# A bias table stored during the first norm and loaded in mid-FFN, and one table padded to 128 bytes

## The reference

```
h = x + 1/2 * SwiGLU_1(RMSNorm(x))            # hidden width 2816
u = RMSNorm(h); one projection of u gives queries, latents, indexer, pool input, 3 gates
h = h + W_out( sum_i sigmoid(gate_i) * (branch_i @ W_branch_i) )
h = h + 1/2 * SwiGLU_2(RMSNorm(h))
```

```python
n = jnp.maximum(dist, 0)                      # below 16: the bucket is the distance
large = 16 + (log(n / 16) / log(128 / 16) * 16).astype(int32)   # at most 31
```

## Time and profile before

| | |
|---|---|
| median of 3 runs | 2397.23 us |
| the profiled execution, its span | 2396.16 us, 2394.3 us |
| mean granted TensorE clock | 0.989 |
| PE busy | 2312.5 us (97%) |
| weight loads (beside PE) | 1846.1 us (77%) |
| DVE, ACT, POOL busy | 52%, 23%, 58% |
| DMA | 208.74 MB, 87 GB/s over the span |

### The profile page before, as it was taken

How to read it: one execution, slowest core, us unless ns; L and a number is a source line. 1 busy time by engine, 2 the same in 40 slices (tenths; PEclk the granted TensorE clock), 3 DMA queues, 4 the chain that set the end, 5 groups by cost and what they waited for, 6 DMA issues and landing times.

```text
span 2394.3 us, 31804 instructions
## 1 busy us (share of the span) xinstructions
PE 2312.5 (97%) x10328; PEld 1846.1 (77%) x10328; DVE 1249.8 (52%) x1756; ACT 560.3 (23%) x1038; POOL 1389.6 (58%) x868
## 2 busy tenths in 40 slices
PE   3999999999999999999999999999999999999997
PEld 2788888777877788888778888877777778888875
DVE  2453355478865755225454524636787566440453
ACT  1211112243455221001121101214334532110111
POOL 2566666634434666666666666664344366666663
PEclk8999999999999999999999999999999999999998
DMA  5233223311121322232232332232121122223222
GB/s 136 90 116 95 97 87 98 101 58 66 58 67 49 112 91 89 88 104 85 81 107 96 110 103 91 80 110 80 54 64 61 53 97 89 97 79 105 96 76 73
DMA packets 66482, 208.74 MB, mean 87 GB/s; under 512 B 7352, under 2 KB 9560, under 8 KB 66136
## 3 DMA queue, kind: packets, MB, share of 16 engines
q1 hardware_dynamic: 63600, 202.84, 25.7%
q10 hardware_dynamic: 2792, 4.72, 0.9%
HBM read 203.86 MB, written 3.67 MB: 87 GB/s over the span
## 4 chain that ended last, share of the span: by engine, by line
PE 89%; DVE 7%; DMA 2%; issue 1%; ACT 1%; DVEq 0%; ACTq 0%
PE bank L517 27%; PE bank L519 27%; PE bank L518 27%; DMA bias_rows<-q 1%; PE obank L737 1%; PE sbank L689 1%; PE tbank L710 1%; DVE u1L L1429 1%; DVE picks L1229 1%; DVE picks L1252 1%; DVE tb L1443 1%; PE sbank L684 1%; PE obank L724 1%; DVE top L1227 1%; PE sbank L671 1%
## 5 line engine op out<-in xcount | busy, mean ns | idle before, releaser
L468 POOL TENSOR_SCALAR wH<-raw 128x1024 fp32r<-128x1024 f32 (+3 forms) x432 | 438.2, 1014 | 944.6 <-PE bank L519 926.8
L471 POOL TENSOR_TENSOR wL<-raw,wH 128x1024 fp32r<-128x1024 f32 (+3 forms) x432 | 951.5, 2202 | 36.0
L517 PE MATMUL bank<-u0H,wH 128*128 128x512 f32 x1408 | 563.3, 400 | 6.9 <-POOL wL L471 4.1
L518 PE MATMUL bank<-u0H,wL 128*128 128x512 f32 x1408 | 559.7, 398 | 0.0
L519 PE MATMUL bank<-u0L,wH 128*128 128x512 f32 x1408 | 559.7, 397 | 0.0
L517 PEld LDWEIGHTS bank<-u0H,wH 128*128 128x128 f32 x1408 | 266.1, 189 | 76.5 <-issue 8.5
L518 PEld LDWEIGHTS bank<-u0H,wL 128*128 128x128 f32 x1408 | 266.4, 189 | 65.3 <-issue 1.2
L519 PEld LDWEIGHTS bank<-u0L,wH 128*128 128x128 f32 x1408 | 266.2, 189 | 65.0
L517 PE MATMUL bank<-u1H,wH 128*128 128x512 f32 x704 | 295.7, 420 | 7.5 <-DVE u1L L1429 3.1
L517 PE MATMUL bank<-hidH,wH 128*128 128x512 f32 x704 | 279.6, 397 | 0.7 <-DVE hidL L1132 0.7
L518 PE MATMUL bank<-hidH,wL 128*128 128x512 f32 x704 | 279.1, 396 | 0.0
(11 more groups left out here) (175 smaller groups left out, 2411.0 us busy)
## 6 DMA issues: line engine op xcount, KB each, us to landing
raw<-in_wA SPq DMA_DIRECT2D x176, 512.0 KB, 3.3
raw<-in_wM SPq DMA_DIRECT2D x96, 512.0 KB, 3.3
raw<-in_wB SPq DMA_DIRECT2D x64, 384.0 KB, 3.0
raw<-in_wB SPq DMA_DIRECT2D x64, 320.0 KB, 2.9
raw<-in_wR SPq DMA_DIRECT2D x32, 256.0 KB, 2.6
h<-in_xT ACTq DMA_DIRECT2D x4, 512.0 KB, 6.8
mem<-in_memT SPq DMA_DIRECT2D x2, 1024.0 KB, 6.8
outT<-gate_a SPq DMA_DIRECT2D x4, 512.0 KB, 2.7
```

The lines of the kernel that those rows point to most:

```text
L468: pool.tensor_scalar(wH[:, w, 0:cols], raw[:, slot, 0:cols], 1.0, 0.0, ALU.mult, ALU.add).then_inc(rounded, 1)
L471: pool.tensor_tensor(wL[:, w, 0:cols], raw[:, slot, 0:cols], wH[:, w, 0:cols].bitcast(F32), ALU.subtract).then_inc(split_done, 1)
L517: pe.matmul(dst, a, hi[:, k, :], start=first and i == 0, stop=False)
L518: pe.matmul(dst, b, hi[:, k, :], start=False, stop=False)
```

## The change

Two things are done. The table's way to DRAM and back is cut up: `hot`, `rel` and the table now lie in the memory of `near_bias`; ACT copies the table after the third tile of the first norm and issues the store after the fourth; the issue of `far_bias` stays after the eighth; the wait for the store and the load of `near_bias` move into the first FFN's code, behind the loop over its first 12 hidden tiles, and so run in both layers (DVE's wait counts accordingly). And `far_bias` is declared 32 words wide instead of 8, so that what is declared after it lies 96 bytes further: `cst` at a multiple of 128 bytes, `pr` 32 past one, `rms` to `sg` 64 past one, `u0H` and all that lay 32 past one at a multiple of 128.

```diff
--- before.py
+++ after.py
@@ -73,6 +73,8 @@
 N_SCORES = 3 * IH
 NBIAS = 384
 
+LINE = 128
+
 
 def attention_steps():
 
@@ -207,7 +209,7 @@
         wH = sb("wH", [P, SPLIT_SLOTS, 8 * P], F32R)
         wL = sb("wL", [P, SPLIT_SLOTS, 8 * P], F32R)
         near_bias = sb("near_bias", [P, H, 2 * P])
-        far_bias = sb("far_bias", [P, H])
+        far_bias = sb("far_bias", [P, LINE // 4])
         cst = sb("cst", [P, N_CONST])
         pr = sb("pr", [P, N_PAR])
         rms = sb("rms", [P, T])
@@ -275,8 +277,10 @@
         ones = cst[:, K_ONE:K_ONE + P]
         causal = cst[:, K_CAUSAL:K_CAUSAL + P]
 
-        rel_sb = q[0:BUCKETS, 1, 0:H]
-        bias_table = q[0:H, 2, 0:NBIAS]
+        bias_scratch = near_bias[:, :, :].rearrange("p a t -> p (a t)")
+        hot_sb = bias_scratch[0:BUCKETS, 0:NBIAS]
+        rel_sb = bias_scratch[0:BUCKETS, NBIAS:NBIAS + H]
+        bias_table = bias_scratch[0:H, 4 * P:4 * P + NBIAS]
 
         def masks(qb):
             return causal if qb == 0 else picks[qb][:, :]
@@ -406,8 +410,8 @@
         def _(sp):
             sp.dma_start(cst[:, :], const).then_inc(const_loaded, 16)
 
-            sp.dma_start(q[0:BUCKETS, 0, 0:NBIAS], hot).then_inc(rel_loaded, 16)
-            sp.dma_start(q[0:BUCKETS, 1, 0:H], rel).then_inc(rel_loaded, 16)
+            sp.dma_start(hot_sb, hot).then_inc(rel_loaded, 16)
+            sp.dma_start(rel_sb, rel).then_inc(rel_loaded, 16)
 
             with sp.Fori(0, L) as l:
                 def units(src, per_layer, first, count, cols, unit):
@@ -537,7 +541,7 @@
 
             pe.wait_ge(const_loaded, 16)
             pe.wait_ge(rel_loaded, 32)
-            pe.matmul(sbank[0][0:H, 0:NBIAS], rel_sb, q[0:BUCKETS, 0, 0:NBIAS], start=True, stop=True
+            pe.matmul(sbank[0][0:H, 0:NBIAS], rel_sb, hot_sb, start=True, stop=True
                       ).then_inc(bias_full, 1)
 
             with pe.Fori(0, L) as l:
@@ -845,19 +849,16 @@
                 if k:
                     act.wait_ge(ssq_added, k)
                 act.activation(sq[:, :], h[:, k, :], ACT.Square).then_inc(squared, 1)
-            act.dma_start(far_bias[:, :], bass.AP(tensor=rel.tensor, offset=(BUCKETS - 1) * H,
-                                                  ap=[[0, P], [1, H]])).then_inc(far_loaded, 16)
-            act.wait_ge(bias_full, 1)
-            act.activation(bias_table, sbank[0][0:H, 0:NBIAS], ACT.Copy).then_inc(bias_copied, 1)
-            act.wait_ge(bias_copied, 1)
-
-            act.dma_start(bias_rows, bass.AP(tensor=bias_table.tensor, offset=bias_table.offset,
-                                             ap=[bias_table.ap[0], [0, P], [1, NBIAS]])).then_inc(bias_stored, 16)
-            act.wait_ge(bias_stored, 16)
-
-            act.dma_start(near_bias[:, :, :], bass.AP(tensor=bias_rows.tensor, offset=P - 1,
-                                                      ap=[[NBIAS - 1, P], [P * NBIAS, H], [1, 2 * P]])
-                          ).then_inc(bias_loaded, 16)
+                if k == 2:
+                    act.wait_ge(bias_full, 1)
+                    act.activation(bias_table, sbank[0][0:H, 0:NBIAS], ACT.Copy).then_inc(bias_copied, 1)
+                if k == 3:
+                    act.wait_ge(bias_copied, 1)
+                    act.dma_start(bias_rows, bass.AP(tensor=bias_table.tensor, offset=bias_table.offset,
+                                                     ap=[bias_table.ap[0], [0, P], [1, NBIAS]])
+                                  ).then_inc(bias_stored, 16)
+            act.dma_start(far_bias[:, 0:H], bass.AP(tensor=rel.tensor, offset=(BUCKETS - 1) * H,
+                                                    ap=[[0, P], [1, H]])).then_inc(far_loaded, 16)
 
             with act.Fori(0, L) as l:
                 def ffn(chunk, hid_from, root_n, hi, g, n_from):
@@ -873,6 +874,10 @@
                     with act.Fori(0, HALF[0] // 2) as j:
                         hidden(j, chunk, hid_from)
                     if chunk == 0:
+                        act.wait_ge(bias_stored, 16)
+                        act.dma_start(near_bias[:, :, :], bass.AP(tensor=bias_rows.tensor, offset=P - 1,
+                                                                  ap=[[NBIAS - 1, P], [P * NBIAS, H], [1, 2 * P]])
+                                      ).then_inc(bias_loaded, 16)
 
                         act.wait_ge(mem_loaded, l * 16 + 16)
                         for k in range(KD):
@@ -1209,7 +1214,7 @@
                     dst = kc[:, i, :] if i < 2 else vc[:, i - 2, :]
                     dve.tensor_copy(dst, bank[i][:, 0:M]).then_inc(evacuated, 1)
 
-                dve.wait_ge(bias_loaded, 16)
+                dve.wait_ge(bias_loaded, l * 16 + 16)
                 dve.wait_ge(far_loaded, 16)
                 mem_kv(0)
                 inverse_rms(l * 5 + 3, tb, D)
```

## The result

The changed kernel takes 2316.72 us, the median of 4 runs (2314.72 to 2317.61), against 2397.55 us of the kernel before in the same rounds (4 runs, 2395.22 to 2398.16): a ratio of 0.9661, 95% interval 0.9649 to 0.9673. That is 80.8 us less; the sum of the prediction had 83.0, 2313 was said and 2303 to 2335 given as the range. The profiled execution took 2316.20 us with a span of 2314.4, which is 80.0 less than the profiled execution of before.

What follows compares the result with a forecast made beforehand. PE's own rate was taken as the bound (busy 97%). 29.6 us from the standstill, 50.4 from matmuls on u0, hid and y and 3 from small ones sum to 83.0, taking 2396.2 to 2313; range 2303 to 2335.

Steps and rivals of the forecast that it cites:

- Part 1, the standstill: At the first norm's spread matmul, issuing the store early removes PE's wait of 29.24 us; 29.6 us gained in sum.
- the issue: On ACT in the first norm, issuing the store delays the next u0H; PE's first unit ends 1.3 us later.
- the margin: At the first spread, diagonals ready at 30.8 and wanted by PE at 35.4: 4.6 us to spare.
- the clock: After the start, without the long pause the granted clock doesn't fall to half; gain 1.7 us.
- The store beside the weights: Early weight tiles land in 16.2 us beside the store, within 18.9 us of slack; cost 0, at most 4 us.
- The load in mid-FFN: The near_bias load behind the first FFN's loop of 12 tiles, in both layers, costs 0; 11 us without cover.
- Part 2, the size: In FFN and mixing stages, 6720 matmuls on u0, hid and y each save 7.5 ns: 50.4 us, lower end 41.7.
- Part 2, the cause: u0, hid and y step at 234.3 ns, u1 at 226.8, because their starts lie 32 past a multiple of 128.
- The first rival: Position of the matmul operands does nothing, u1's rate comes from something else: 2366.6 us, chance 0.11.
- the fourth: Rival: in the FFN, operands on wH's and wL's multiple collide with GpSimd's writes; slower, 2405 us, chance 0.02.
- The rule of the 16-byte line: For SBUF accesses only 16-byte lines count, so 32 past a multiple of 128 is fine and padding gives 0.
- The small rest: Mixing stage's small matmuls and 256-column ones on mem gain 3 us from the padding, bounds -5 to +9.

Runs made afterwards that it cites:

- padding alone: The kernel before with far_bias declared 32 words wide and nothing else: 2346.84 us against 2397.67 (ratio 0.9795).
- early store alone: The kernel after with far_bias declared 8 words wide again: 2365.60 us (ratio 0.9869 to the kernel before).
- all 32 off: The kernel after with 32 bytes left free ahead of h, so every tensor lies 32 bytes further: 2317.04 us against 2399.07 before.
- the small kernel: A separate kernel of matmul runs at varied row and weight starts, no other engine computing; 128 columns took 111.7 ns a step at distances 0 and 160.
- weights 32 off: The kernel after with 32 bytes left free ahead of wH and 96 behind wL: 2365.95 us against 2399.07 before.

## Why the prediction was right, and where not

**What bounds the kernel.** Right: each ns a step came back as time. 6336 matmuls x 7.6 ns are 48 us on u0 and hid, and the four rows of the table that hold them are 47.4 us shorter with the padding alone.

**Part 1, the standstill.** Right in its mechanism. 29.6 us were forecast; the stretch to the first hid matmul is 28.8 us shorter with the early store alone (186.8 to 158.0), the medians say 32.1, the profiled executions 30.0. The terms: the standstill of 29.24 is gone whole. For the issue 1.3 were forecast and 1.4 measured in one pair. For the margin 4.6 us were forecast and 36.50 - 32.93 = 3.57 measured, in a profile whose first matmul was 0.5 late. What was missed in it: the issue of far_bias, which was costed as hidden at its 0.33 us, took 4.14, since it stood on the queue behind the store; it held the root until 29.39, 0.85 us after the variance. In the profile of the change the clock did what was said: it is 1.00 over the whole first layer. That isn't so in each execution: with the early store alone it was at 0.77 in the mean from 15 to 30 us, where PE still goes at the pace of the tiles, and none of them has the long fall of the earlier trace rows.

**The store beside the weights.** Right at 0. Landing times of 16.6 us and less met a slack of 18.1, and without the store PE's stretch has the same length to the hundredth.

**The load in mid-FFN.** Right at 0, in 6.7 us to land.

**Part 2, the size.** Right to 3 us: 50.4 us forecast for 6720 matmuls and 3 for the rest, 53.4 in all; 50.8 measured for the padding alone.

**Part 2, the cause.** Wrong. The step of the prediction was "what differs and would explain it is the start of the operand": u0, hid and y 32 past a multiple of 128, u1 on one. The runs show that the start by itself does nothing (all 32 off: 226.7), and that the distance from the weights makes the difference between these operands. That the forecast came out all the same is luck: it did because u1 was both on a multiple of 128 and at distance 0, and because 96 bytes turn a distance of 160 into 256. For 128 bytes more of padding the same reasoning would have said 50 us again, and the chip gave 14 (45.8 less than before, of which the early store is 32.1). The first rival ("position does nothing") was half the truth and wrongly tied to no gain; the fourth, a collision with GpSimd's writes of the weights, named the right partner with the wrong sign and the wrong engine.

**The rule of the 16-byte line.** The Trainium skill ("SBUF — State Buffer", Door 1) counts 16-byte lines. By that rule the padding would have given nothing and the time 2366.6, and the runs disagree: multiples of 16 give rates from 226.7 to 234.6. The same page ("Who interferes with whom") has PE read moving operand and weights over two independent ports. In the kernel before with the weights moved, u0 and hid keep their place modulo 256 while the weights move by 160 bytes, and a step changes by 7.6 ns, which is hard to square with ports that are independent in every respect; where the two meet, no run shows.

**The small rest.** Here a term was mis-sized: 3 us were put on the mixing stage's small matmuls, and they gave nothing that shows. Both stages together shrank by 4.9 from before to after. By the starts in the two traces 1.2 of it lie in y's 384 matmuls (2.9 were forecast, as part of the 50.4), 0.9 in steps on u1, whose own rate in the long stretch is unchanged, and 2.2 in the 256-column matmuls on the memory tokens at the stages' head. The 128-column matmuls took the same time to 0.1 us, as in the small kernel. The 2.2 us go with the granted clock rather than the place: before it was 0.91 from 425 to 445 us and 0.83 from 1585 to 1605, around those matmuls of the two layers; after, it was 1.00 from 385 to 405 and 0.91 from 1520 to 1540. The early store alone, unpadded, took 9.9 us for the 48 matmuls of layer 1 with a fall of the clock (0.93 from 385 to 410 us) and 8.4 for those of layer 2 without one. The last 0.6 us stand at one sum over rows in layer 2.

## What to carry to other kernels

Where PE is the bound and rows of 512 float32r columns from starts at multiples of 32 bytes are streamed, look at the steps from start to start in a long unbroken stretch, by operand; if operands differ by some ns, compare their distances from the weights in SBUF modulo 256 before their positions, and pad until the distance is a multiple of 256. A comparison between two tensors of one trace gave the size of the gain well here and its cause badly, since they differ in more than one thing; one run that moves all tensors together and one that moves only the weights tell. And a wait on an engine's queue costs what stands behind it: take the wait for a long DMA away from the first thing on the critical path, and look also at what the next DMA on that queue takes to issue.

## What the runs showed of the hardware

In these runs a step of 512 columns was 226.7 to 227.0 ns only where row and weights started at multiples of 32 and a multiple of 256 bytes apart, and in the one run with the row 240 past the weights; the fourteen other multiples of 16 gave 228.9 to 234.6. The slowest were rows that start 4 bytes past a multiple of 16 with the weights at 0: 236.6 and 240.0. Behind smaller matmuls that step is reached after eight uneven ones (233, 236, 224, 231, 236, 228, 232, 231). Why the distance matters at all, and why 240 is fast and both at 16 isn't, stays open; no whole kernel tried 240.

The issue of a DMA isn't of fixed length. That of far_bias took 0.33 us with nothing large ahead on its queue. Behind the store (8 heads x 128 copies of 1536 bytes) it took 3.8 to 4.4 us in the six executions in which it began 6.3 us after the store's, and 1.23 us in the one in which it began 7.6 us after (weights 32 off). So the issue behind the large store seems to wait for a part of it, and less when it comes later. Weight tiles issued beside that store landed after up to 16.6 us, with 3.3 elsewhere, though the DMA engines were 43% idle from 20 to 55 us.

The granted clock falls to 0.50 for 3.4 or 6.8 us in some executions and not in others, at the same short waits. This is one window of the kernel after in its two profiled executions, the second as run again (us, busy by engine, clock, DMA share, GB/s):

```profile
385.00:400.00 15.00, 12.73 (x97) 11.89 (x98) 7.75 (x16) 2.73 (x4) 12.31 (x8) 1.00 0.35 121
```

```profile
385.00:400.00 15.00, 12.73 (x76) 11.78 (x75) 7.21 (x15) 2.64 (x4) 9.95 (x6) 0.77 0.31 105
```

The mixing stage of layer 1 took 410.5 us in the one and 415.0 in the other, while the two executions differ by 3.3 us as a whole. That is as much as the runs of one kernel spread, and the reason that a difference of 1 us has to be read from the timeline of the stretch that it concerns.
